# One block for rows, index projections, scores, projections and latents, with short-format products

## The reference

```python
(c_q, c_kv, k_r, q_b, k_b, v_b, q_i, k_i, w_i, gate_a, gate_b) = jnp.split(h @ w_in, offs, axis=-1)
q_a = (rmsnorm(c_q, g_cq) @ w_uq)          # latents: 256 columns
kv_a = (rmsnorm(c_kv, g_ckv) @ w_ukv)      # latents: 128 columns
k_rope = rope(k_r[:, :, None, :], pos)     # 32 columns
...
logits = jnp.einsum('bqhd,bkd->bqhk', qib, k_i)              # 8 index heads of 64
score = jnp.einsum('bqh,bqhk->bqk', wb, jax.nn.relu(logits))
_, idx = lax.top_k(score, k_sel)                             # 256 keys a query
```

## Time and profile before

| | |
|---|---|
| median of 3 runs | 1633.92 us (1629.78 to 1636.15) |
| profiled execution | 1635.34 us, span 1633.4 us |
| mean granted clock of TensorE | 0.938 |
| TensorE busy | 1434.7 us, 88% of the span |
| VectorE busy | 1052.9 us, 64% |
| ScalarE busy | 650.6 us, 40% |
| GpSimd busy | 405.3 us, 25% |

### The profile page before, as it was taken

How to read it: one execution, slowest core, us unless ns; L and a number is a source line. 1 busy time by engine, 2 the same in 40 slices (tenths; PEclk the granted TensorE clock), 3 DMA queues, 4 the chain that set the end, 5 groups by cost and what they waited for, 6 DMA issues and landing times. The chain is left out here.

```text
span 1633.4 us, 21404 instructions
## 1 busy us (share of the span) xinstructions
PE 1434.7 (88%) x7182; PEld 1108.7 (68%) x7191; DVE 1052.9 (64%) x2047; ACT 650.6 (40%) x1129; POOL 405.3 (25%) x406
## 2 busy tenths in 40 slices
PE   6996899999999898988889888999945999999960
PEld 3465688889895457777667666889944777777730
DVE  4158999999922466666676665443254777777737
ACT  3157212121211236666666654021103666666622
POOL 1000322221211105454434411410002233333213
PEclk9998899999999999999999998999966999999985
DMA  7450122332231000302323204423154899999808
GB/s 195 51 87 14 58 81 87 103 97 91 73 117 42 1 0 1 72 1 66 75 60 82 66 1 161 157 87 104 65 219 182 321 357 357 356 367 376 328 31 319
DMA packets 86604, 216.82 MB, mean 133 GB/s; under 512 B 23720, under 2 KB 46792, under 8 KB 74232
## 3 DMA queue, kind: packets, MB, share of 16 engines
q1 hardware_dynamic: 76152, 194.72, 36.4%
q0 software_dynamic: 9216, 16.80, 2.8%
q10 hardware_dynamic: 1152, 4.19, 0.6%
HBM read 187.75 MB, written 44.70 MB: 142 GB/s over the span
## 5 line engine op out<-in xcount | busy, mean ns | idle before, releaser
L1193 DVE TENSOR_TENSOR pL<-ps,pH 128x512 fp32r<-128x512 f32 (+3 forms) x224 | 127.0, 574 | 114.4 <-ACT pH L1130 113.6
L457 DVE TENSOR_SCALAR_CACHE_REDUCE mask<-score,cand 128x272 bf16<-128x272 f32 (+6 forms) x224 | 185.5, 892 | 5.0 <-DVE cand L476 4.9
L2102 DVE TENSOR_TENSOR w_rest<-wgu,w_lead 128x1024 fp32r<-128x1024 f32 x128 | 156.0, 1223 | 45.0 <-ACT w_lead L2049 43.8
L542 PE MATMUL ps<-hHi,g_lead 128*128 128x512 f32 (+2 forms) x416 | 158.6, 381 | 16.2 <-DVE hLo L582 16.2
L543 PE MATMUL ps<-hLo,g_lead 128*128 128x512 f32 (+2 forms) x416 | 158.8, 382 | 0.0
L544 PE MATMUL ps<-hHi,g_rest 128*128 128x512 f32 (+2 forms) x416 | 158.0, 380 | 0.0
L2049 ACT CAST w_lead<-wgu 128x1024 fp32r<-128x1024 f32 x128 | 134.4, 1055 | 37.9 <-PE ps L1995 37.9
L1130 ACT CAST pH<-ps 128x512 fp32r<-128x512 f32 (+3 forms) x224 | 107.7, 488 | 71.5 <-PE ps L1078 70.5
L1993 PE MATMUL ps<-w_lead,x_lead 128*128 128x512 f32 x256 | 114.2, 446 | 6.0 <-DVE w_rest L2102 6.0
L577 POOL TENSOR_TENSOR g_rest<-g_raw,g_lead 128x2048 fp32r<-128x2048 f32 x13 | 61.7, 4745 | 227.8 <-ACT g_lead L551 227.8
L2015 PE MATMUL ps<-wd,hmT 128*128 128x512 f32 x256 | 115.3, 593 | 1.6 <-DVE hmT L2125 1.0
(11 more groups left out here) (332 smaller groups left out, 3453.1 us busy)
## 6 DMA issues: line engine op xcount, KB each, us to landing
wgu<-in_w_exp_gate SPq DMA_DIRECT2D x32, 1024.0 KB
wgu<-in_w_exp_up SPq DMA_DIRECT2D x32, 1024.0 KB
wd<-in_w_exp_down SPq DMA_DIRECT2D x32, 1024.0 KB
g_raw<-in_w_in SPq DMA_DIRECT2D x14, 1024.0 KB, 5.5
gates_d<-stage SPq DMA_DIRECT2D x32, 256.0 KB, 2.0
gt<-gates_d SPq DMA_DIRECT2D x32, 256.0 KB, 3.2
rel_d<-relf SPq DMA_DIRECT2D x1, 4672.0 KB
KR<-kb_d SPq DMA_DIRECT2D x16, 260.0 KB, 6.0
```

The lines of the kernel that those rows point to most:

```text
L457: return dve.tensor_scalar(mask[:, OFF[i]:OFF[i + 1]], score[:, OFF[i]:OFF[i + 1]], thr, 0.0, op, ALU.add, accum_out=cnt[:, i:i + 1])
L542: pe.matmul(dst, x[0], y[0], start=(k == 0), stop=False)
L1193: dve.tensor_tensor(pL[n % RING][:, lo:512], bank_of(k)[:, lo:512], pH[n % RING][:, lo:512].bitcast(F32), ALU.subtract).then_inc(s_rs, 1)
L2102: dve.tensor_tensor(w_rest[u][:, :, 2 * part:2 * part + 2, :], wgu[u][:, :, 2 * part:2 * part + 2, :], w_lead[part][:, :, :, :].bitcast(F3 ...
```

## The change

The first three blocks and the latents of the fourth become one program block.

- The rows are scaled by the gain before the transposes (gmixb, loaded as a broadcast) and written straight to hHi by ScalarE and to hLo by VectorE. hT is gone, and so are the later splits.
- The index queries become pieces 0 and 1 of w_in, in the same two buffers as the others; the index keys and weights have a small piece of their own (kw_raw). All index jobs are 24 short-format products. The first four need only the first four row blocks, and the transposes of the other blocks stand between them.
- The gates are now pieces 2 to 9. SyncE issues pieces 2 and 3 after index jobs 6 and 8; ScalarE casts piece 2 after the eighth index output and piece 3 after the tenth.
- The first four gate jobs are cut into eight parts of three products, one after every second score step. The score ring has three positions of two banks instead of four, then two of three; wide scores are cut into even chunks.
- The latents are 24 short-format products a block, one block after each of the jobs 10 to 18, their transposes two blocks later. ScalarE copies and squares, GpSimd normalises and rotates, ScalarE writes the transposed rows with the gains.
- The rotary rows of the keys are no longer copied to each head; ScalarE and VectorE write them once into both buffers KH and KL, and the head keys are split in 64 rows instead of 96.
- Queries, keys and values follow in the same block.

```diff
-        hT = at("hT", [P, KT, L], F32, R_H)
+        hHi = at("hHi", [P, KT, L], F32R, R_H)
+        hLo = at("hLo", [P, KT, L], F32R, R_Q)
...
+        piece_col = ([C_QI, C_QI + 256] + [c + 256 * k for c in (C_GA, C_GB) for k in range(4)]
+                     + [c + 256 * k for c in (C_VB, C_QB, C_KB) for k in range(2)])
...
+        EARLY, LATE = 4, 10
+        items = []
+        for n in range(len(jobs)):
+            items.append(("job", n))
+            b = n - LATE
+            if 0 <= b < 9:
+                items.append(("lr", b))
+            if 2 <= b < 11:
+                items.append(("tr", b - 2))
+        def step_at(n):
+            return (1024 * (n % 3) if n < WIDE else 1536 * (n % 2)) + chunks(WID[steps[n][0]])[0]
...
             def _(sp):
+                rows_in(0)
+                sp.dma_start(gmixb[:, :], a["norm_mix_g"].to_broadcast([P, D])).then_inc(s_gb, 16)
+                sp.dma_start(con[:, :], a["const"]).then_inc(s_con, 16)
+                rows_in(1)
+                rows_in(2)
+                piece_in(0)
+                rows_in(3)
...
+                rows_in(4)
+                piece_in(1)
+                for b in range(5, 9):
+                    rows_in(b)
+                    sp.dma_start(kw_raw[:, :, :], w_in[:, :, C_KI:C_KI + 72]).then_inc(s_kww, 16)
...
+                sp.wait_ge(s_relc, 1)
+                sp.dma_start(rel_d, relf[:, :].unsqueeze(1).to_broadcast([H, P, REL])).then_inc(s_reld, 16)
+                for p in range(2):
+                    sp.wait_ge(s_ij, 6 + 2 * p)
+                    piece_in(p + 2)
                 for n, (kind, p, t, (lo, hi)) in enumerate(jobs):
+                    if n == EARLY:
+                        sp.wait_ge(s_lg, NSTEP)
+                        sp.dma_start(lr_raw[:, :, :], w_in[:, :, 0:LR]).then_inc(s_lrw, 16)
...
             def _(pe):
+                def three(dst, x, y, k):
+                    pe.matmul(dst, x[0], y[0], start=(k == 0), stop=False)
+                    pe.matmul(dst, x[0], y[1], start=False, stop=False)
+                    return pe.matmul(dst, x[1], y[0], start=False, stop=(k == KT - 1))
...
+                for n in range(len(idx_jobs)):
+                    idx_job(n)
+                    if n < 4:
+                        transposes(4 + n)
+                    if n == 3:
+                        transposes(8)
...
+                for n, (i, h) in enumerate(steps):
+                    if n >= 3:
+                        pe.wait_ge(s_re, n - 2 if n < WIDE else n - 1)
+                    o = step_at(n)
+                    for part, keys in enumerate((KiHi, KiLo)):
+                        for lo, hi in chunks(WID[i])[1]:
+                            mm = pe.matmul(flat[:, o + lo:o + hi], Qi2[:, h, P * i:P * (i + 1)],
+                                           keys[:, lo:hi], start=(part == 0), stop=(part == 1))
+                    mm.then_inc(s_lg, 1)
+                    if n % 2 == 1:
+                        q, k = divmod(n // 2, KT)
+                        job(q, q, [k])
+                pe.wait_ge(s_re, NSTEP)
+                for q in range(EARLY, NI):
+                    kind, n = items[q]
+                    if kind == "job":
+                        job(q, n, range(KT))
+                    elif kind == "lr":
+                        latents(q, n)
+                    else:
+                        latent_rows(q, n)
...
             def _(act):
                 def lead(p):
                     act.wait_ge(s_gws[p % 2], 16 * (p // 2 + 1))
+                    if p >= 2:
+                        act.wait_ge(s_wl, p - 1)
                     act.copy(g_lead[p % 2][:, :, :], g_raw[p % 2][:, :, :]).then_inc(s_wh, 1)
...
+                for n in range(len(idx_jobs)):
+                    idx_out(n)
+                    if n == 7:
+                        lead(2)
+                    if n == 9:
+                        lead(3)
+                for n, (i, h) in enumerate(steps):
...
+                    if n % 16 == 15:
+                        job_out(n // 16, n // 16)
...
             def _(pool):
+                    if b == 3:
+                        rest(0)
+                    if b == 6:
+                        rest(1)
...
+                for b in range(9):
+                    while p < NP and p <= at_job[b] + 1:
+                        rest(p)
+                        p += 1
+                    latents_norm(b)
...
             def _(dve):
+                    dve.scalar_tensor_tensor(xn[b % 2][0:r, :], xb[b % 4][0:r, :], rstd[0:r, b:b + 1],
+                                             gmixb[0:r, :], ALU.mult, ALU.mult).then_inc(s_xn, 1)
...
+                for k in range(2):
+                    dve.tensor_tensor(KL[k][NOPE:QKD, :], krT[NOPE:QKD, :], KH[k][NOPE:QKD, :].bitcast(F32),
+                                      ALU.subtract).then_inc(s_h1, 1)
```

More of the change, by code:

```diff
@@ L173, in hybrid_layer @@
         top = keep("top", 2)
+        R_OT = small[0]
         otok = [keep(f"otok{k}", 4 * P) for k in range(2)]
@@ L198, in hybrid_layer @@
[L198 to L202, removed]
+        xb = [at(f"xb{k}", [P, D], F32, R_X + 4096 * k) for k in range(4)]
+        sqj = at("sqj", [P, D], F32, R_X + 16384)
@@ new lines, in hybrid_layer @@
+        rt = [at(f"rt{k}", [P, L], F32, R_X + 4160 * k) for k in range(4)]
+        stage = [at(f"stage{k}", [P, 512], F32, R_I + 41088 + 2048 * k) for k in range(4)]
+        assert R_I + 41088 + 8192 <= R_M
+        kw_raw, kw_rest = (at(nm, [P, KT, 72], dt, R_I + 41088) for nm, dt in (("kw_raw", F32), ("kw_rest", F32R)))
+        kw_lead = at("kw_lead", [P, KT, 72], F32R, R_I + 41088 + 2304)
+        g_raw, g_rest, g_lead = ([at(f"g_{nm}{k}", [P, KT, 256], dt, R_W + 16384 * k + off) for k in range(2)]
+                                 for nm, dt, off in (("raw", F32, 0), ("rest", F32R, 0), ("lead", F32R, 8192)))
@@ new lines, in hybrid_layer @@
+        thirds = [(0, 352), (352, 704), (704, L)]
+        jobs = ([("gate", p, t, c) for p in range(2, 10) for t in range(2) for c in halves]
+                + [("v", p, t, (P * t, min(L, P * (t + 1)))) for p in (10, 11) for t in range(9)]
+                + [("q", p, t, c) for p in (12, 13) for t in range(2) for c in halves]
+                + [("k", p, t, c) for p in (14, 15) for t in range(2) for c in thirds])
+        last_job = {p: n for n, (_, p, _, _) in enumerate(jobs)}
+        first_job = {p: n for n, (_, p, _, _) in reversed(list(enumerate(jobs)))}
@@ new lines, in latent_rows @@
+                def latent_rows(q, b):
+                    r, bank = rows[b], item_bank(q)
+                    pe.wait_ge(s_ge, q - 7)
+                    pe.wait_ge(s_ln, b + 1)
+                    for k in range(0 if b < NB else 2, 3):
+                        pe.transpose(ps[:, bank, P * k:P * k + r], lrn[b % 2][0:r, P * k:P * (k + 1)], ident[0:r, 0:r])
+                    pe.transpose(ps[0:96, bank, 384:384 + r], krx[b % 2][0:r, :], ident[0:r, 0:r]).then_inc(s_gj, 1)
+                pe.wait_ge(s_con, 16)
@@ new lines, in latent_rows_out @@
+                def latent_rows_out(q, b):
+                    r, bank = rows[b], ps[:, item_bank(q), :]
+                    act.wait_ge(s_gj, q + 1)
+                    if b < NB:
+                        for k in range(2):
+                            act.activation(cqT[:, k, P * b:P * (b + 1)], bank[:, P * k:P * (k + 1)], ACT.Copy,
+                                           scale=gcq[:, k:k + 1]).then_inc(s_lc, 1)
+                    act.activation(ckvT[:, cols[b]:cols[b] + r], bank[:, 256:256 + r], ACT.Copy,
+                                   scale=gckv[:, 0:1]).then_inc(s_lc, 1)
+                    act.copy(krT[NOPE:QKD, cols[b]:cols[b] + r], bank[NOPE:QKD, 384:384 + r]).then_inc(s_ge, 1)
@@ new lines, in _ @@
+                act.wait_ge(s_gain, 32)
+                act.wait_ge(s_sc, NSTEP)
+                for q in range(EARLY, NI):
+                    kind, n = items[q]
+                    if kind == "job":
+                        job_out(q, n)
+                        if n == EARLY + 1:
+                            act.wait_ge(s_lrw, 16)
+                            act.copy(lr_lead[:, :, :], lr_raw[:, :, :]).then_inc(s_lrh, 1)
+                    elif kind == "lr":
+                        latents_out(q, n)
+                    else:
+                        latent_rows_out(q, n)
@@ L879, in _ @@
                 q_out(dve, NB - 1)
+                for k in range(4):
+                    dve.wait_ge(s_gds[k], 16 * len(range(k, len(jobs), 4)))
                 for n in range(1, len(kv_jobs), 2):
```

919 lines of the change are left out of this document (431 added, 488 removed).

## The result

| | median | runs | range |
|---|---|---|---|
| before | 1631.85 us | 4 | 1626.76 to 1636.15 |
| after | 1616.92 us | 4 | 1616.59 to 1617.47 |

The ratio is 0.991, 95% interval 0.9889 to 0.9931: faster by 0.9%, more than the 0.5% that a measurement can tell. The profiled execution took 1617.06 us (forecast 1617.1), with a span of 1615.3 us and a mean granted clock of 0.936.

The account below looks back on a forecast made before the run. TensorE was taken to bound nearly everything up to 559 us. The query stage starting 17.6 us earlier plus 0.6 gave 1635.3 - 18.2 = 1617.1 us for the profiled execution (1616 on the median's scale), range 1604 to 1628.

Parts of the forecast that it names:

- Part 1: Rows and index projections: 56 us of products against 72, starting at 24 to 28 us, ending at 88 to 98; outside the sum.
- the stall: Before the scores: loads of pieces 2 and 3 held up behind the bias-table store rel_d, taking back 40 us of gain.
- the rival without it: Loads not held up: they land within 10 us, scores start near 97, everything after 40 us earlier, 1576; chance 0.10.
- Part 2: Wait before the scores: piece 2 lands at 127.0, ScalarE's queue waits, scores start at 137.0 instead of 104.5; bounds 133 to 141.
- Part 3: Scores with four gate jobs between: TensorE bounds them, 61.8 us in total, leaving at 198.8; bounds 54 to 68.
- the rival of a half clock throughout: Scores: TensorE stays at 1.2 GHz, 57.5 us become 115, 54.7 more, 1671 in all; chance 0.06.
- The 1 us for the lock: Scores: one more microsecond because VectorE and GpSimd exclude each other, piece 3's remainder overlapping the first scores.
- the 2.75 us of half clock: Start of the scores: TensorE's clock at half for 5.5 us after idle time, costing 2.75 us.
- Part 4: Splits between scores and jobs: 18.5 us gone; VectorE's selection starts about 202 instead of 174, ends near 485, delay covered.
- Part 5: Jobs and latents on TensorE: 297.1 us of jobs, 41.0 latents, 4.4 transposes; ends at 541.3; bounds +0 to +8.
- nearer 4.3: Latents' normalisation on GpSimd: under 7.6 us a block, nearer 4.3, in a period of 10.6 us.
- Part 6: Query stage: VectorE starts the first query block at 546.3 against 563.92, 17.6 us earlier; the second block saves 0.6.

Follow-up runs that it names:

- x2_two_step: Changed kernel with the bias table stored once, then copied 128 times HBM to HBM with outer dimension 128 instead of 8: 1585.39 us, ratio 0.9708.
- x3_act_queue: Changed kernel with the same store of the bias table (rel_d) issued by ScalarE instead of SyncE: 1619.70 us, ratio 0.9919.
- x4_before_two_step: Kernel before the change with the same two-step copy of the bias table as x2_two_step: 1631.77 us against 1632.73, ratio 0.9994.
- x9_late46: Changed kernel with the nine latent blocks after jobs 46 to 54 instead of 10 to 18: 1623.91 us, ratio 0.9955.
- the last experiments: x11_lead_back beside x12_rest_again, five rounds on one chip, also compared with x6_rest_dve on another: medians 1575.17 and 1579.72 us, against 1579.56.
- x12_rest_again: Second run of the unchanged x6_rest_dve kernel, beside x11_lead_back on the same chip: 1579.72 us, ratio 0.968.
- x6_rest_dve: x2_two_step with the remainders of pieces 0 and 1 on VectorE instead of GpSimd: 1579.56 us, ratio 0.9675.
- x11_lead_back: x6_rest_dve with index outputs 0 to 2 taken between the row blocks instead of after all rows: 1575.17 us, ratio 0.9652.

## Why the forecast came out

**Part 1, rows and index projections.** Direction right, size low. The jobs ran from 28.04 to 100.2, where 88 to 98 was the forecast for the end. Missing were two operations of VectorE in the row stage, each 4.2 us longer by the lock that I had weighed only for the scores, and about 3 us lost at half clock after TensorE's pauses near 45 and 62. It cost nothing in the result, for the stall covered it; it is why the stall was worth 32 us and not 40, and why the rival without it would have been 1585 and not 1576.

**Part 2, the new wait.** Right in every link that counts: rel_d's issue 1.0 later than estimated, piece 2 at 127.15, scores from 137.22. One link was missing: the issue of piece 3 itself was held up for 28.71 us, so that no half of it went through at once. It landed in time for its cast and cost nothing. x2_two_step shows that rel_d is the cause, x3_act_queue that a load on another queue is held up too, x4_before_two_step that before the change it was free. The rule of the Trainium skill, "DMA: Bandwidth & Descriptors", section on why a DMA increments its semaphore by 16, agrees: outer dimension 8 gave a share of 0.49 to 0.50, outer dimension 128 gave 1.03.

**Part 3, scores.** 198.89 - 137.22 = 61.7 against 61.8, with 5.8 us at half clock. That TensorE would be the bound there was right, and the rival of a half clock throughout fell: 0.99 from 143 on. But two things in the sum are luck. The 1 us for the lock was nothing: piece 3's remainder on GpSimd ran from 133.87 to 138.38, and VectorE's first score operation with two inputs came at 140.45, at its usual 0.37 us; 61.7 less 2.9 for the clock and 0.4 for the last Relu leaves 58.3 for the products and their small waits, where 57.5 was taken, and the two errors cancel. And the 2.75 us of half clock came, but the long idleness that was given as its reason isn't needed: x2_two_step has the same 5.8 us after a wait of 2.50.

**Part 4, the splits.** Gone, and the later selection was covered: counting starts at 200.93 and ends near 481, sixty microseconds before TensorE.

**Part 5, jobs and latents.** 541.20 - 198.89 = 342.3 against 342.5. The GpSimd chain took 3.85 us a block, under the forecast's "nearer 4.3". x9_late46 shows how much this depends on the place: among VectorE's scans the same chain takes 10.1 us, and TensorE waits for the last block, which stands behind a remainder in GpSimd's list.

**Part 6, query stage.** 546.20 against 546.3. The span from there on is 1069.1 us, before it was 1069.5.

The close agreement is partly luck: besides the terms of part 3, versions of this program differ by 3 us in stretches that no edit touches, and two executions of one kernel, on two chips, by 2.2 us at the first query copy, as the last experiments show.

## What to carry to other kernels

A wait costs what stands behind it in program order, not what needs the data: before a cast or copy is put into an engine's list, look up when its transfer lands and whose work it delays. Read each large transfer's share of the DMA engines in a fine window; one at half share for 95 us held up the later loads that are spread over all of them, on its own queue and on another. And when a long-hidden transfer gets a new neighbour, change the transfer first: here a few lines of it were worth twice the whole change.

## What was unexpected of the hardware

- A store repeated from 8 partitions moved 51 GB/s, and the 4672 KB took some 95 us. Through a small copy in HBM and an outer dimension of 128 they took 18.2 us at 300 GB/s. Twice the engines explain only a factor of two of the 5.2.
- A transfer on ScalarE's queue held up one on SyncE's by 64 us (67.5 against 3.3), and SyncE's issues of kw_raw and the two small loads behind it took 4.79, 6.98 and 11.09 us, against 0.43, 0.58 and 0.47 in the changed kernel. In the changed kernel itself, piece 3's issue behind rel_d took 28.71 us.
- VectorE and GpSimd exclude each other at whole instructions: 1.28 us became 5.52 beside a GpSimd operation of 4.50, 0.37 became 4.58 beside one of 4.55, and a GpSimd operation of 0.23 became 2.07 beside a scan of 2.06. The Trainium skill, "SBUF — State Buffer", section on SBUF's two separate sides, says this of a VectorE operation with two SBUF inputs and a GpSimd operation that reads SBUF. The VectorE operations in all three cases have two, and the counting beside which GpSimd kept its 0.23 has one. Two inputs aren't the whole condition in these traces: beside VectorE's comparison at 467.66, which has one large input, a GpSimd operation of 0.22 us took 0.55.
- TensorE's clock after a pause isn't the same even in one kernel: behind a wait of 2.50 us it stayed at 1.00 in x12_rest_again and fell in x6_rest_dve, whose kernel is the same, on another chip, and in x11_lead_back on the chip of x12_rest_again (0.50 and 0.76 in the windows above).
